# Pairing the modulation pieces of a trunk kernel's first attention: one bank, one copy and one set of transposes for two pieces

## What is computed

```
def ada_mod(cond, w_ada_l, b_ada_l):
    m = jax.nn.silu(cond) @ w_ada_l + b_ada_l
    m = m.reshape(cond.shape[0], 1, N_MOD, D_MODEL)
    return [m[:, :, i] for i in range(N_MOD)]
...
    sh1, sc1, gt1, sh2, sc2, gt2 = ada_mod(c, w_ada[l], b_ada[l])
    h = rms_norm(z, g_attn[l]) * (1 + sc1) + sh1
    ...
    z = z + gt1 * merge_heads(o_na, o_mla, o_swa, w_out[l])
    h = rms_norm(z, g_ffn[l]) * (1 + sc2) + sh2
    z = z + gt2 * moe(h, w_router, b_router, w_gate[l], w_up[l], w_down[l])
```

## Time and profile before

| what | value |
|---|---|
| median of 3 runs | 1121.33 us (1119.64 to 1124.69) |
| the profiled execution | 1123.75 us, span 1121.7 us |
| PE, DVE, ACT busy | 1060.4, 848.9, 688.0 us |
| mean granted TensorE clock | 0.984 |
| first attention, first scores to first output projection | 128.8 to 212.1 us of the span |

### The profile page before, as it was taken

One profiled execution on the slowest core, in us unless ns is written; L12 is line 12 of the kernel. 1 busy time (PEld: TensorE's weight loads), 2 busy tenths in 40 slices (PEclk: granted clock), 3 DMA queues, 4 the chain that ended last, 5 costly groups with the idle time before them and its releaser, 6 DMA issues.

```text
span 1121.7 us, 16007 instructions
## 1 busy us (share of the span) xinstructions
PE 1060.4 (95%) x5943; PEld 839.7 (75%) x5943; DVE 848.9 (76%) x1191; ACT 688.0 (61%) x867; POOL 158.2 (14%) x184
## 2 busy tenths in 40 slices
PE   6999999897999999999989999898899999999996
PEld 3698555683888888888868986577488888888876
DVE  5255556668899888888955547866889988988896
ACT  2323555544677777777724256754468777777863
POOL 0226200320011111111040011000111111111002
PEclk8999999998999999999999999999899999999999
DMA  9997899246999999999599463005599999999941
GB/s 348 346 332 214 314 314 322 79 165 256 372 355 370 370 377 373 373 381 385 216 367 270 150 191 127 1 1 196 220 387 362 386 370 379 382 370 369 368 191 58
DMA packets 82560, 319.86 MB, mean 285 GB/s; under 512 B 22464, under 2 KB 26926, under 8 KB 69692
## 3 DMA queue, kind: packets, MB, share of 16 engines
q1 hardware_dynamic: 67232, 285.58, 69.6%
q0 software_dynamic: 14160, 30.19, 7.9%
q10 hardware_dynamic: 1100, 3.23, 0.7%
HBM read 308.05 MB, written 30.57 MB: 302 GB/s over the span
## 4 chain that ended last, share of the span: by engine, by line
PE 81%; issue 7%; DVE 6%; ACT 2%; DMA 2%; POOL 0%; SPq 0%; DVEq 0%; ACTq 0%; POOLq 0%
PE bank L1219 16%; PE bank L1211 16%; PE bank L1212 16%; PE bank L1104 3%; PE bank L927 3%; PE bank L931 3%; PE bank L924 3%; PE bank L1270 2%; PE bank L901 2%; PE bank L1118 2%; PE bank L996 2%; PE bank L1136 2%; DMA ring<-in_w_ada 2%; PE bank L1037 1%; PE bank L1300 1%
## 5 line engine op out<-in xcount | busy, mean ns | idle before, releaser
L1673 ACT ACTIVATE work_r<-ring 128x4096 fp32r<-128x4096 f32 x93 | 338.1, 3636 | 120.2 <-PE bank L1212 108.8
L2259 DVE TENSOR_TENSOR ring_r<-ring,work_r 128x4096 fp32r<-128x4096 f32 x92 | 404.2, 4418 | 5.7 <-ACT work_r L1673 5.7
L1211 PE MATMUL bank<-work_r 128*128 128x512 f32 x768 | 306.4, 399 | 4.5 <-issue 4.2
L1212 PE MATMUL bank<-work_r 128*128 128x512 f32 x768 | 301.5, 393 | 0.0
L1219 PE MATMUL bank<-ring_r,work_r 128*128 128x512 f32 x768 | 193.8, 395 | 0.0
L1211 PEld LDWEIGHTS bank<-work_r 128*128 128x128 f32 x768 | 145.4, 189 | 35.3 <-issue 5.0
L1219 PEld LDWEIGHTS bank<-ring_r,work_r 128*128 128x128 f32 x768 | 143.8, 188 | 32.2
L1212 PEld LDWEIGHTS bank<-work_r 128*128 128x128 f32 x768 | 145.2, 189 | 28.8
L2522 POOL DMA_INDIRECT work<-hscr,idx x32 | 38.8, 1214 | 360.3 <-PE bank L1270 248.7
L1529 ACT ACTIVATE work_r<-ring 128x512 fp32r<-128x512 f32 (+1 forms) x48 | 28.8, 603 | 71.6 <-PE bank L931 71.5
L1953 DVE TENSOR_TENSOR ring_r<-ring,work_r 128x512 fp32r<-128x512 f32 (+1 forms) x48 | 32.2, 677 | 51.5 <-ACT work_r L1529 51.3
(11 more groups left out here) (270 smaller groups left out, 1534.4 us busy)
## 6 DMA issues: line engine op xcount, KB each, us to landing
ring<-in_w_gate SPq DMA_DIRECT2D x32, 2048.0 KB, 10.5
ring<-in_w_up SPq DMA_DIRECT2D x32, 2048.0 KB, 11.0
ring<-in_w_down SPq DMA_DIRECT2D x32, 2048.0 KB, 10.5
ring<-in_w_ada SPq DMA_DIRECT2D x24, 2048.0 KB, 10.4
ring<-in_w_in SPq DMA_DIRECT2D x4, 2048.0 KB, 15.3
yscr<-hT POOLq DMA_DIRECT2D x2, 3072.0 KB, 13.0
ring<-yscr SPq DMA_DIRECT2D x6, 1024.0 KB, 7.3
ring<-in_w_out SPq DMA_DIRECT2D x4, 1280.0 KB, 7.0
```

The lines of the kernel that those rows point to most:

```text
L1211: mm(b[:], x_hi[:, k, :], hi[:, k, half, :], start=(k == 0), stop=False)
L1212: last = mm(b[:], x_lo[:, k, :], hi[:, k, half, :], start=False, stop=False)
L1673: A_(w_hi[:, slot % 2, :], ring[slot][:], ACT.Copy).then_inc(s_hi, 1)
L2259: tt(ring_r[slot][:], ring[slot][:], w_hi[:, slot % 2, :].bitcast(F32), ALU.subtract).then_inc(s_lo, 1)
```

## The change

The ten pieces of `ADA_ATT` become five pairs. The first piece of a pair is the new job `F`: the same 8 matmuls as an `A`, which open the accumulation in bank 7 and leave it open. The second piece, in the next step, is the pair's `A`: its 8 matmuls add into the same bank, with the two silu columns shifted to columns 2 and 3 of the 32 (`sil32_second`; the buffer `sil34` has two zero columns ahead of the silu columns, and both views of it are 32 wide). So rows 0 and 1 of each band hold the first piece, rows 2 and 3 the second. One copy to `arow`, one set of four transposes (`B`) follow for both. DVE reads the result with two reductions and adds one bias of twice the width.

The places: pair p (0 to 4) has `F` in step 4p + 1, `A` in step 4p + 2, nothing in step 4p + 3 and `B` in step 4p + 4. Step 0 has no ada job any more, and the last `B` is in step 20 in place of 19. ACT takes its order "exps first" only in the five steps with an `A`. The slot of a first piece is released by a semaphore of its own, `s_adafirst`.

```
+ADA_PAIRS = list(zip(ADA_ATT[0::2], ADA_ATT[1::2]))
+ADA_TURNS = ADA_FIRST + [b for _, b in ADA_PAIRS] + ADA_ROUTE[0] + ADA_GAP + ADA_ROUTE[1]
...
 def ada_in_step(i):
 
-    return [f"{'AB'[i % 2]}{x}{c}" for x, c in ADA_ATT[i // 2:i // 2 + 1]]
+    pair, place = divmod(i - 1, 4)
+    if not 0 <= pair < len(ADA_PAIRS) or place == 2:
+        return []
+    (x1, c1), (x2, c2) = ADA_PAIRS[pair]
+    return [(f"F{x1}{c1}", f"A{x2}{c2}", None, f"B{x2}{c2}")[place]]
...
-        sil32 = sb("sil32", [P, KT, 32])
+        sil34 = sb("sil34", [P, KT, 34])
+        sil32, sil32_second = sil34[:, :, 2:34], sil34[:, :, 0:32]
...
+        def read_by(sp, reader):
+
+            firsts = [(0, "A{}{}".format(*x)) for x, _ in ADA_PAIRS]
+            if reader in firsts:
+                sp.wait_ge(s_adafirst, firsts.index(reader) + 1)
+            else:
+                is_filled(sp, reader)
...
-                    if kind == "A":
+                    pair = [p for p in ADA_PAIRS if (x, c) in p]
+                    if kind in "FA":
                         w = arrived(pe, l, ("ada", x, c)).rearrange("p (k n) -> p k n", k=KT)
-                        b = fill_begin((l, j))
-
+                        opens, closes = kind == "F" or not pair, kind == "A"
+                        whole = (l, "A{}{}".format(*pair[0][1])) if pair else (l, j)
+                        b = fill_begin(whole) if opens else bank(whole)
+
+                        sil_ = sil32 if opens else sil32_second
                         for k in range(KT):
-                            last = mm(b[32 * (k % 4):32 * (k % 4) + 32, :], sil32[:, k, :], w[:, k, :], start=(k < 4), stop=(k >= 4),
-                                      skip_group_check=True)
+                            last = mm(b[32 * (k % 4):32 * (k % 4) + 32, :], sil_[:, k, :], w[:, k, :], start=(opens and k < 4),
+                                      stop=(closes and k >= 4), skip_group_check=True)
+                        if not closes:
+                            last.then_inc(s_adafirst, 1)
+                            return
...
-            nc.vector.memset(sil32[:, :, 2:32], 0.0)
-            tt(sil32[:, :, 0:2].rearrange("p k c -> p c k"), sil[:, 0, :].rearrange("p (c k) -> p c k", c=2),
+            nc.vector.memset(sil34[:, :, 0:2], 0.0)
+            nc.vector.memset(sil34[:, :, 4:34], 0.0)
+            tt(sil34[:, :, 2:4].rearrange("p k c -> p c k"), sil[:, 0, :].rearrange("p (c k) -> p c k", c=2),
...
+                    n = 2 if any((x, c) == p[1] for p in ADA_PAIRS) else 1
+                    c -= n - 1
                     b = take(v, (l, j))
-                    mod = modT[:, x, 4 * c:4 * c + 4, :]
-                    partial = b[:].rearrange("p (j g r) -> p j r g", j=4, g=4)[:, :, 0:2, :]
-                    evac((l, j), nc.vector.tensor_reduce(mod, partial, AX.X, ALU.add))
+                    for i in range(n):
+                        mod = modT[:, x, 4 * (c + i):4 * (c + i) + 4, :]
+                        partial = b[:].rearrange("p (j g r) -> p j r g", j=4, g=4)[:, :, 2 * i:2 * i + 2, :]
+                        ins = nc.vector.tensor_reduce(mod, partial, AX.X, ALU.add)
+                    evac((l, j), ins)
                     read_out(v, (l, j))
-                    tt(mod, mod, vT[:, 0, x * 48 + 4 * c:x * 48 + 4 * c + 4].unsqueeze(2).to_broadcast([P, 4, 2]), ALU.add)\
-                        .then_inc(s_mod, 1)
+                    mod = modT[:, x, 4 * c:4 * (c + n), :]
+                    bias = vT[:, 0, x * 48 + 4 * c:x * 48 + 4 * (c + n)]
+                    tt(mod, mod, bias.unsqueeze(2).to_broadcast([P, 4 * n, 2]), ALU.add).then_inc(s_mod, n)
```

More of the change, by code:

```diff
@@ L202, in job_order @@
             n += ENTRY.get(i, [])
-            n += ada_in_step(i) if l == 0 else []
+            n += [j for j in ada_in_step(i) if j[0] != "F"] if l == 0 else []
             if 0 <= i - LAG_T < NS:
@@ L458, in build @@
         s_mod = sem("s_mod")
+        s_adafirst = sem("s_adafirst")
         s_sq = sem("s_sq")
@@ L682, in chunk @@
                 if k >= SLOTS:
-                    is_filled(sp, last_reader(l, k - SLOTS))
+                    read_by(sp, last_reader(l, k - SLOTS))
                 elif l > 0:
@@ L754, in before @@
                         if p == 0:
-                            is_filled(sp, last_reader(l, MOE_AT[l] - SLOTS + slot))
+                            read_by(sp, last_reader(l, MOE_AT[l] - SLOTS + slot))
                         else:
@@ L1493, in ada_row @@
                 if j[0] == "A":
-                    before = ADA_ALL.index((int(j[1]), int(j[2:]))) - 1
+                    before = ADA_TURNS.index((int(j[1]), int(j[2:]))) - 1
                     if before >= 0:
-                        x = ADA_ALL[before]
+                        x = ADA_TURNS[before]
                         is_filled(act, (ADA_LAYER[x], "B{}{}".format(*x)))
```

## The result

The changed kernel takes 1114.70 us (median of 20 runs, 1111.71 to 1118.46), the kernel before 1121.44 us (median of 20 runs beside them). The ratio is 0.9941, with a 95% interval of [0.9932, 0.995]: 6.7 us faster by the medians, where 3.5 were forecast. The profiled execution took 1112.73 us.

A forecast was written before the change was run, and what follows sets the result against it. PE was taken to bound the first attention, though not alone; 2.3 us of transposes plus 1.25 us of waits made about 3.5 us, taking the median from 1121.33 to 1117.8 us, range 1114.7 to 1122.3.

The forecast's parts named there:

- all that is behind it keeps its length: Sign to look for: everything after the first attention takes as long as before, with only that stage shrinking, 83.3 to 79.8 us.
- the clock: Rival: earlier start moves a low-clock stretch behind the attention off or onto matmuls, 1.7 us: 1116.1 or 1119.5; 0.07 each.
- all waits go: Rival: bank and norm waits in the first attention vanish and its tail gains 0.46; gain 4.9 us, 1116.4; chance 0.05.
- the sets: First attention: five sets of four transposes removed from PE at 0.46 us each, saving 2.3 us.
- the waits: First attention: PE's waits for bank 7 and `arow`, 2.1 us, become 0.85 us of other waits; gain 1.25 us.
- ACT and DVE have over 30 us of idle time in the stage, so these are worth nothing: First attention: five removed ACT copies, five small adds and one wait per pair save nothing by themselves.
- Waits for bank 7: First attention: `F` waits for DVE to release the bank, 0.15 us at step 9 and 0.35 at step 13.
- The turn at step 12: First attention: behind a `B`, the turn waits 0.35 us for a norm, the only `B` step where it does.
- The tail: Last `B` moves to step 20, covers 0.46 of step 21's 0.82 us wait; its DVE work gives that back: nothing net.
- Light steps that stall at 0.81 each: Rival: ten steps with nothing or a `B` each wait 0.81 us for DVE; 3.7 us slower, 1125.0; chance 0.08.
- No gain: Rival: PE's freed time in the first attention turns into waits for DVE's norms; 1121.3; no or little gain 0.17.
- The ring: First pieces free their slots a step, about 3.5 us, later; 27 us of slack, so no cost, else 3.5 us once.

The follow-up runs named there:

- e2: Kernel before with only the silu buffer widened to 34 columns, shifting everything allocated behind it by 64 bytes; ratio 0.9965 to the kernel before, stage 83.27 us.
- e3: The change with its buffer allocated last and an empty one of the old size in the old place, so no other tensor moves; ratio 0.9982, stage 80.56 us.
- e12: The change with the four transposes of each pair done twice, five sets more at the same places; one run, read by its stage: 81.66 us.
- e8: The change with ACT's copy of turned weights put ahead of its copy to `arow`; ratio 0.9942 to the kernel before, stage 79.60 us.
- e1: The kernel before once more, unchanged; ratio 0.9999, stage 84.42 us.
- e7: The kernel before with 64 empty bytes just ahead of `work`, nothing else moved; ratio 0.9968.
- e4: The change with `F` in step 4p, `A` in 4p + 2, `B` in 4p + 3, places of the old schedule; ratio 0.993 to the kernel before, stage 80.32 us.

## Why the prediction was off by half of the gain

**The step that failed** is "all that is behind it keeps its length". The forecast took the wider buffer into account for its own matmuls alone ("shifted columns or not, since both views are 32 columns wide", which held). It followed every instruction that the change moves, and no address. The line of the diff that makes `sil32` two columns wider per chunk also shifts `work` onto the ring's place modulo 256 bytes, and 768 matmuls that read both get 4 ns shorter. That wide buffer alone is worth 3.9 us of the 6.6 that the ratio gives (e2), more than the intended part. None of the rivals had it. Those nearest in their number, the clock with 1116.1 and "all waits go" with 1116.4, were not the cause. That the range reached down to 1114.7 is luck: it added a clock term of 1.7 us to all waits going, and e3 shows that the waits didn't go. The forecast gave 0.10 to a gain of more than 5.6 us.

**The stage was mis-sized** by 0.8 us, with its mechanism right in the sets and wrong in the waits: 83.27 to 80.56, 2.7 for a forecast of 3.5. The sets gave 2.2 of it, near the 2.3 forecast. The waits gave 0.5 where the sum had 1.25: all of PE's waits in the stage add up to 5.6 us before and to 5.1 in e3.
- The sets: 0.43 to 0.46 each, as forecast. Five are 2.2 us of PE, but e12 shows that putting five back costs 1.1, for most of the rest lies in waits. Price and worth are different things.
- The missing term: three turns wait 0.55 + 0.27 + 0.42 = 1.24 us for ACT's turned copy. "ACT and DVE have over 30 us of idle time in the stage, so these are worth nothing" was true as an average; in a step with an `A`, ACT is late at one moment, and that one releases PE. With the term out (e8) the stage is 79.60, near the forecast 79.8.
- Waits for bank 7: 0.31 at step 9 against 0.15. The forecast set its chain of 2.25 against a cover of 2.1, where its own working at step 12 had 2.0 from the end of the scores; with that it would have had 0.25. At step 13 the rows leave 0.10 us between the end of the scores (164.69 + 0.92 = 165.61) and the `F` at 165.71, against 0.35. The sum is 0.4 against 0.5.
- The turn at step 12: at most 0.11 against 0.35, since the wait for ACT two rows ahead had already let the norm catch up; 0.23 once that wait is away (e8).
- The tail: the forecast's "nothing net" holds, with two waits of 0.38 and 0.43 in place of the 0.82 of the earlier trace rows.
- The `B`'s waits for `arow`, 0.5: gone, as forecast.

**The rivals.** Light steps that stall at 0.81 each: no such row; three of the ten do stall, for 0.27 to 0.55 us, and for ACT. No gain: refuted by e3, whose interval ends at 0.9991, though its mechanism takes half of each set. The clock: it did dip at the stage's tail, for about 1.2 us (81.82 against 80.56), but so did the kernel before in e1 (84.42 against 83.27), and e8 has it in its second attention (62.44 against 61.26): it comes with either schedule. The other dip, at the end of the first layer's experts, is near the forecast's 1.7 us in size, but not by an earlier start: e3 has the new schedule and keeps it, e2 has the old one and is without it. The ring, a step later, cost nothing, as forecast.

**What stays open.** Why matmuls care for the distance of their two tensors: the runs show that they do, not by what. Why the matmuls with both operands in `work_r` gain 0.4 ns too. Why the second attention, which has no ada job, is 0.23 us shorter in the kernels with the changed schedule (61.26 in e3) and not with padding alone (61.49 in e7); it lies in one wait for ACT, of the scores of step 3: 0.73 us in e1, 0.42 in e3. Whether the low clock at the end of the first layer's experts has to do with the layout: all seven traces with a distance of 64 to 192 have it, and of the seven with distance 0 only e4 and e12, whose first experts take 289.7 and 289.5 us for it. Whether e8 beats the change: 1 us in the stage, nothing that five runs could tell in the total.

## What to carry to other kernels

When a diff changes the size of any buffer, list what is allocated behind it and run the kernel before with that size alone: here this control explains more of the gain than the edit itself, and 64 bytes of padding give 0.3% without touching the schedule. Price removed work by its row, and then look at what is late at that place next: half of it may have been filling a wait, and the shares of busy time don't tell. Two profiled executions of one kernel can differ by 4 us in stages that nothing touched, so compare by stage, and each stage over several executions.

## What the runs showed of the hardware

- The time of the experts' matmuls of 128x512, with the moving operand in the ring and the stationary one in `work`, goes by the distance of the two tensors modulo 256 bytes: eight take 1.818 us at 0, 1.851 at 192, 1.864 at 128, 1.867 at 64, at a granted clock of 1.00. From best to worst that is 2.7%, and in this kernel 0.64% of the time (0.9968 to 1.0032). For the projections' matmuls of 128x384, with the operands the other way round, the order is another: 173.7 ns at 64, 174.3 at 0, 176.3 at 192, 176.6 at 128. Other pairs of tensors were not tried on purpose.
- The granted clock can be 0.66 on average over the last 5 us of the attention in one execution and stay at 1.00 in the next (e3) of the same schedule; it costs 1.2 us.
